# Norms and transposes by column halves in a fused two-block transformer kernel

## The chip, the cores and the metric

The kernel runs on one core of one Trainium2 chip. The metric is the time of one execution on the device in microseconds (us), as the median of several runs; lower is better.

## The reference

Two transformer blocks run one after the other on 256 tokens of 1024 channels, in float32. What matters here is that every product over the 1024 channels is preceded by a normalisation of each token over its channels, and by a transposition into feature form.

```python
h = rmsnorm(x, norm_mix_w) * (1.0 + sc1) + sh1      # stage "mix"
x = x + g1 * (concat(hgrn2(h @ w_in), attention, conv) @ w_out)
h = rmsnorm(x, norm_mlp_w) * (1.0 + sc2) + sh2      # stage "mlp"
x = x + g2 * (square(relu(h @ mlp_w1)) @ mlp_w2)
x = rmsnorm(x, final_norm_w)                        # stage "fin"
for i in range(2):                                  # layers 0 and 1
    x = layer_norm(ALPHA * x + mixer_i(x), ln1_g[i], ln1_b[i])          # "ln1_i"
    x = layer_norm(ALPHA * x + swiglu(x, w1, w3, w2), ln2_g[i], ln2_b[i])  # "ln2_i"
    x = x + sigmoid(x @ ple_w_gate[i] + ple_b_gate[i]) * (p[i] @ ple_w_proj[i])
```

## The kernel before

The residual x lies in SBUF as two token halves of 128 partitions with 1024 columns each (`x[:, t, :]`, t = 0 or 1), and its normalised form in `xn` likewise. The weights come as one stream of tiles of 128 x 2048 float32 (1 MB), five slots deep; SyncE issues them in a fixed order, each into the slot that the products have given free. For precision each product is made of three: ScalarE rounds a tile to `w_hi` (line 1122), VectorE subtracts to get `w_lo` (line 1514), the input is split in the same way into `hT_hi` and `hT_lo` (lines 1531, 1532), and TensorE adds up hi x hi, hi x lo and lo x hi (lines 582, 587, 588). The order of each engine's instructions is written out by hand; counting semaphores link the engines, and a list of the uses of the eight PSUM banks sets the order in which they are filled (`psum_full` counts them one by one).

Ahead of eight of the groups of products stands a seam with always the same steps:

- VectorE computes 1 / root of the mean square (`rstd`, with ScalarE's square root between), then normalises the two token halves with one `tensor_scalar` of 1024 columns each: line 1565 for the RMS norm (stages mix, mlp, fin), line 1946 for the layer norm (ln1 and ln2 of both layers). Each adds one to `xn_ready`.
- TensorE (`to_feature_form`, lines 650 to 662) waits for token half t, then transposes its eight blocks of 128 columns into four PSUM banks, two blocks into each. Bank j holds columns 256 j to 256 j + 255 of both token halves, so it is full when the second half has been transposed into it. Line 657 is the transposition.
- ScalarE (`evacuate`) takes the banks in order and copies each with scale and shift into the arena, two instructions of 256 columns (line 1107; line 1105 in stage ple, which has no scale).
- VectorE (`split_transposed`) takes each pair of chunks that ScalarE has made and splits it (lines 1531 and 1532).
- TensorE starts the first product as soon as the first pair is split, and goes by chunks in the first tile, so that it can follow the splits one by one.

In the seam "ple", between layer 0 and layer 1, there is no normalisation: x itself is transposed, after the last addition of line 2114. In the layer-norm seams VectorE has a weight tile (`lo_ahead(tile, 0)`) to split between normalisation and input split, if it has not done so earlier; behind the input split it splits the next weight tile and then scales and shifts x itself (lines 1956 and 1959; 1903 in stage fin). ScalarE rounds weight tiles ahead (`ahead`) at fixed places between its other work; in stage mix two of them come right before the evacuation (line 1199).

Of the kernel before, what the change touches and what calls it, by code (L numbers as in the profile page):

```python
# [24 lines left out]
ALU = mybir.AluOpType  # L25
# [3 lines left out]
P = 128  # L29
T = 256  # L30
TT = T // P
# [283 lines left out]
def build(nc, x_in, wstream, pcol_in, prow_in, const_in, p_in, out):  # L315
    ctx = ExitStack()
    with ctx:
# [22 lines left out]
        x = sb("x_res", [P, TT, D])  # L340
        xn = sb("xn", [P, TT, D])
# [26 lines left out]
        ident = const[:, CONST["ident"]:CONST["ident"] + P]  # L368
# [91 lines left out]
        stat = tiny[:, 80:96]  # L460
# [8 lines left out]
        mv = tiny[:, 164:172]  # L469
# [17 lines left out]
        psum_full = sem("psum_full")  # L487
# [9 lines left out]
        xn_ready, fin_scaled = sem("xn_ready"), sem("fin_scaled")  # L497
# [56 lines left out]
        def _(pe):  # L554
# [95 lines left out]
            def to_feature_form(stage, n):  # L650

                banks = [begin("tr", stage, j) for j in range(4)]
                for t in range(TT):
                    pe.wait_ge(xn_ready, TT * (n - 1) + t + 1)
                    for j in range(4):
                        for c in range(2):
                            last = nc.tensor.transpose(  # L657
                                banks[j][:, c * T + t * P:c * T + (t + 1) * P],
                                (x if stage == "ple" else xn)[:, t, (2 * j + c) * P:(2 * j + c + 1) * P], ident)
                        if t == TT - 1:  # L660
                            last.then_inc(psum_full, 1)
                chunks(DC)

            def modulation(u):
# [157 lines left out]
            for t in range(TT):  # L822
                K = (t + 1) * P
                for j in range(4):
                    b = begin("sc", t, j)
                    r = 32 * j
                    for hh in range(2):
                        last = mm(b[:, hh * K:(hh + 1) * K],
                                  iqT[r:r + 32, hh * T + t * P:hh * T + (t + 1) * P],
                                  ikT[r:r + 32, 0:K], start=True, stop=True)  # L830
# [6 lines left out]
            for h in range(4):  # L837
                last = mm(b[:, h * P:(h + 1) * P], A_hg[:, h * T:h * T + P], v_hg[:, h * P:(h + 1) * P],
                          start=True, stop=True)
            last.then_inc(psum_full, 1)  # L840
            b = begin("hgo", 1)
            for h in range(4):
                mm(b[:, h * P:(h + 1) * P], A1_hg[:, h * P:(h + 1) * P], v_hg[:, h * P:(h + 1) * P],
                   start=True, stop=False)
                last = mm(b[:, h * P:(h + 1) * P], A_hg[:, h * T + P:(h + 1) * T],
                          v_hg[:, 512 + h * P:512 + (h + 1) * P], start=False, stop=True)
# [3 lines left out]
            for c in range(2):  # L850
# [5 lines left out]
                for j in range(31):  # L856
                    last = mm(b[:, 0:T], tap_matrix(c, j), hpad[:, c * 286 + j:c * 286 + j + T],
                              start=j == 0, stop=j == 30)
# [5 lines left out]
            for c in range(2):  # L864
                last = mm(b[:, 0:T], avg[:, :], conv[:, c * T:(c + 1) * T], start=c == 0, stop=c == 1)
            last.then_inc(psum_full, 1)
            for t in range(TT):
                pe.wait_ge(o_normed, t + 1)
                b = begin("hgt", t)
                for h in range(4):  # L870
                    last = nc.tensor.transpose(b[:, h * P:(h + 1) * P],
                                               q_hg[:, t * 512 + h * P:t * 512 + (h + 1) * P], ident)
# [3 lines left out]
            for c in range(2):  # L876
                last = mm(b[:, 0:T], avg[:, :], conv[:, c * T:(c + 1) * T], start=c == 0, stop=c == 1)
# [41 lines left out]
            for layer in range(2):  # L919
                if layer == 0:  # L920
# [6 lines left out]
                    for j in range(2):  # L927
# [3 lines left out]
                        for c in range(2):  # L931
                            for t in range(TT):
                                last = nc.tensor.transpose(
                                    b[:, c * T + t * P:c * T + (t + 1) * P],
                                    xn[:, t, (2 * j + c) * P:(2 * j + c + 1) * P], ident)
# [15 lines left out]
                    for t in range(TT):  # L951
                        for n in range(2):
                            b = begin("uq", t, n)
                            m = 512 if n == 0 else 256
                            for k in range(2):
                                x_ready(k, 4)
                                last = product3(b[:, 0:m], x_part(k, t * P, (t + 1) * P),
                                                (vh[:, k, n * 512:n * 512 + m], vl[:, k, n * 512:n * 512 + m]),
                                                k == 0, k == 1, first)
# [4 lines left out]
                    for j in range(4):  # L964
                        b = begin("uk", j)
                        for o in range(2):
                            for k in range(2):
                                x_ready(2 + k, 4)
                                c = (2 * j + o) * 64
                                last = product3(b[0:64, o * T:(o + 1) * T], (vh[:, k, c:c + 64], vl[:, k, c:c + 64]),  # L970
                                                x_part(2 + k), k == 0, k == 1, first)
                        last.then_inc(psum_full, 1)
                    for n in range(2):
                        b = begin("uv", n)
                        for t in range(TT):
                            for k in range(2):
                                c = 512 + n * T
                                last = product3(b[:, t * T:(t + 1) * T], x_part(2 + k, t * P, (t + 1) * P),
                                                (vh[:, k, c:c + T], vl[:, k, c:c + T]), k == 0, k == 1, first)
# [3 lines left out]
                    for t in range(TT):  # L983
                        last = nc.tensor.transpose(b[0:96, t * P:(t + 1) * P], krtok[:, t * 96:(t + 1) * 96], ident)
# [502 lines left out]
        def _(dve):  # L1487
            step = [0]
            V = nc.vector
# [30 lines left out]
            def own(s, n=1):  # L1520

                made[s.name] = made.get(s.name, 0) + n
                dve.wait_ge(s, made[s.name])
# [32 lines left out]
            def rms_norm(n, pieces=1):  # L1556
                dve.wait_ge(squares_summed, n)
                squares = ssum[:, 0:TT]
                if pieces > 1:
                    squares = stat[:, 4:4 + TT]  # L1560
                    link(V.tensor_reduce(squares, ssum[:, 0:TT * pieces].rearrange("p (t n) -> p t n", t=TT), AX.X,
                                         ALU.add))
                rstd(TT, 1.0 / D, EPS, squares)
                for t in range(TT):
                    V.tensor_scalar(xn[:, t, :], x[:, t, :], stat[:, 8 + t:9 + t], None, ALU.mult)\
                        .then_inc(xn_ready, 1)
                own(xn_ready, TT)

            def softmax(name, heads, base, bias, scale, c0, beside, tiles):
                us = units(heads)  # L1570
# [367 lines left out]
            def layer_norm(g_row, b_row, stage, layer, tile, pieces):  # L1938

                for t in range(TT):  # L1940
                    last = V.bn_aggr(mv[:, 2 * t:2 * t + 2],
                                     bn[:, 24 * t:24 * t + 6 * pieces].rearrange("p (a b) -> p a b", a=pieces))
                link(last)
                rstd(TT, 1.0, EPS_LN, mv[:, 0:4].rearrange("p (t e) -> p t e", e=2)[:, :, 1])
                for t in range(TT):
                    V.tensor_scalar(xn[:, t, :], x[:, t, :], mv[:, 2 * t:2 * t + 1], stat[:, 8 + t:9 + t],
                                    ALU.subtract, ALU.mult).then_inc(xn_ready, 1)
                own(xn_ready, TT)

                lo_ahead(tile, 0)  # L1950
                split_transposed(stage)
                lo_ahead(tile, 1)
                if g_row == 0:
                    dve.wait_ge(lay_loaded, 16 * (layer + 1))
                for t in range(TT):
                    last = V.tensor_tensor(x[:, t, :], xn[:, t, :], lay_row(g_row), ALU.mult)
                link(last)
                for t in range(TT):
                    last = V.tensor_tensor(x[:, t, :], x[:, t, :], lay_row(b_row), ALU.add)
                link(last)  # L1960

            for layer in range(2):
# [164 lines left out]
                            last.then_inc(x_done, 1)  # L2127
                last = gated(3)
                if layer == 0:
                    last.then_inc(xn_ready, TT)  # L2130
                    own(xn_ready, TT)
                    lo_ahead("ff")
                    split_transposed("ple")
                else:
                    last.then_inc(x_done, 1)
                    own(x_done, 4)
# [134 lines left out]
```

## Time and profile before

| | |
|---|---|
| median of 3 runs | 1299.59 us (1299.54 to 1299.69) |
| profiled execution | 1301.13 us |
| its span, from first to last instruction | 1299.3 us |
| TensorE busy (matmuls) | 1163.6 us, 90% of the span |
| VectorE busy | 754.8 us, 58% |
| ScalarE busy | 546.4 us, 42% |
| granted TensorE clock, mean | 0.934 of full |

The span is what the trace shows of the profiled execution; 1.8 us of its time lie around it. In the rows below PE is TensorE, PEld its weight loads, DVE VectorE, ACT ScalarE; bank, arena, xn and so on are the program's own names of buffers. A granted clock of 1.00 is 2.4 GHz, of 0.50 is 1.2 GHz. What a row calls idle is the time the engine had nothing to run, with the instruction whose end released it.

### The profile page before, as it was taken

The page shows a single profiled execution, that of the slowest core. Times are in us where ns is not written, and L with a number is a line of the kernel's source. Part 1 is how long each engine was busy: PE and PEld are TensorE (multiplying, and loading weights), DVE is VectorE, ACT ScalarE, POOL GpSimd, SP SyncE. Part 2 cuts the span into 40 slices and gives each one's busy share as a digit, 9 for nine tenths or more (in the row PEclk, how much of TensorE's full clock was granted, in tenths as well). Part 3 has the DMA queues.
Part 4 walks back from the last instruction along what each step waited for, and adds up shares of the span by engine and source line. Part 5 has one row for each costly group of instructions (what it writes and reads, how often), then busy time and mean ns, then how long its engine had stood idle before and what let it go on. Part 6 is the DMA issues. An engine that isn't in the chain of part 4 may idle for free.

```text
span 1299.3 us, 18592 instructions
## 1 busy us (share of the span) xinstructions
PE 1163.6 (90%) x7908; PEld 1045.8 (80%) x7908; DVE 754.8 (58%) x932; ACT 546.4 (42%) x755; POOL 0.2 (0%) x4
## 2 busy tenths in 40 slices
PE   4879989779999989947879999987999979999997
PEld 2879778559998879946679998886987659999887
DVE  2565556756775455366575665486344457566557
ACT  4562227244443334384543333344444444333333
POOL 0000000000000000000000000000000000000000
PEclk7788999888999998978999999998998979999999
DMA  9522764123555535410235555535431115455551
GB/s 387 229 83 98 287 229 177 61 90 132 193 180 185 193 128 215 150 66 33 98 118 176 194 176 184 193 130 211 147 114 68 63 67 183 175 193 177 192 182 34
DMA packets 33698, 200.95 MB, mean 155 GB/s; under 512 B 3152, under 2 KB 4688, under 8 KB 11984
## 3 DMA queue, kind: packets, MB, share of 16 engines
q1 hardware_dynamic: 32048, 190.30, 40.3%
q10 hardware_dynamic: 1568, 9.46, 1.9%
q8 instruction: 63, 1.03, 0.3%
q14 instruction: 19, 0.16, 0.0%
HBM read 198.70 MB, written 1.05 MB: 154 GB/s over the span
## 4 chain that ended last, share of the span: by engine, by line
PE 71%; DVE 16%; ACT 6%; DMA 4%; issue 2%; ACTq 0%; SPq 0%; DVEq 0%
PE bank L582 21%; PE bank L587 20%; PE bank L588 20%; DMA raw<-wstream 4%; DVE w_lo L1514 4%; PE bank L771 2%; DVE hT_lo L1532 2%; ACT w_hi L1122 1%; PE bank L1030 1%; DVE hT_hi L1531 1%; PE bank L764 1%; PE bank L1029 1%; PE bank L657 1%; PE bank L706 1%; PE bank L674 1%
## 5 line engine op out<-in xcount | busy, mean ns | idle before, releaser
L1514 DVE TENSOR_TENSOR w_lo<-raw,w_hi 128x2048 fp32r<-128x2048 f32 (+1 forms) x159 | 358.2, 2257 | 191.6 <-ACT w_hi L1122 184.5
L1122 ACT ACTIVATE w_hi<-raw 128x2048 fp32r<-128x2048 f32 (+1 forms) x159 | 299.4, 1885 | 280.0 <-PE bank L582 237.7
L582 PE MATMUL bank<-hT_hi,w_hi 128*128 128x256 f32 (+1 forms) x1360 | 392.5, 289 | 20.0 <-DVE w_lo L1514 11.0
L587 PE MATMUL bank<-hT_lo,w_hi 128*128 128x256 f32 (+1 forms) x1360 | 390.0, 287 | 0.0
L588 PE MATMUL bank<-hT_hi,w_lo 128*128 128x256 f32 (+1 forms) x1360 | 389.5, 286 | 0.0
L582 PEld LDWEIGHTS bank<-hT_hi,w_hi 128*128 128x128 f32 (+1 forms) x1360 | 264.9, 195 | 24.5 <-DVE w_lo L1514 12.5
L587 PEld LDWEIGHTS bank<-hT_lo,w_hi 128*128 128x128 f32 (+1 forms) x1360 | 265.1, 195 | 0.1
L588 PEld LDWEIGHTS bank<-hT_hi,w_lo 128*128 128x128 f32 (+1 forms) x1360 | 264.8, 195 | 0.2
L582 PE MATMUL bank<-w_hi,hT_hi 128*128 128x256 f32 (+3 forms) x448 | 148.3, 331 | 32.0 <-DVE w_lo L1514 12.1
L587 PE MATMUL bank<-w_lo,hT_hi 128*128 128x256 f32 (+3 forms) x448 | 144.3, 322 | 0.0
L588 PE MATMUL bank<-w_hi,hT_lo 128*128 128x256 f32 (+3 forms) x448 | 143.7, 321 | 0.0
L582 PEld LDWEIGHTS bank<-w_hi,hT_hi 128*128 128x128 f32 x448 | 92.6, 207 | 42.7 <-issue 18.6
L582 PE MATMUL bank<-w_hi,hid_hi 128*128 128x512 f32 x304 | 118.3, 389 | 0.0
L587 PE MATMUL bank<-w_lo,hid_hi 128*128 128x512 f32 x304 | 118.3, 389 | 0.0
L588 PE MATMUL bank<-w_hi,hid_lo 128*128 128x512 f32 x304 | 118.3, 389 | 0.0
L588 PEld LDWEIGHTS bank<-w_hi,hT_lo 128*128 128x128 f32 x448 | 92.2, 206 | 5.0
L587 PEld LDWEIGHTS bank<-w_lo,hT_hi 128*128 128x128 f32 x448 | 92.7, 207 | 4.2
L587 PEld LDWEIGHTS bank<-w_lo,hid_hi 128*128 128x128 f32 x304 | 57.1, 188 | 11.8
L582 PEld LDWEIGHTS bank<-w_hi,hid_hi 128*128 128x128 f32 x304 | 57.1, 188 | 11.8
L588 PEld LDWEIGHTS bank<-w_hi,hid_lo 128*128 128x128 f32 x304 | 57.1, 188 | 11.8
L1147 ACT ACTIVATE arena<-arena,tiny 128x128 f32<-128x128 f32 (+1 forms) x56 | 25.0, 447 | 72.0 <-DVE tiny L1592 71.9
L1465 ACT ACTIVATE arena<-bank 128x512 f32<-128x512 f32 x22 | 13.1, 597 | 78.0 <-PE bank L588 78.0
(264 smaller groups left out, 1099.4 us busy)
## 6 DMA issues: line engine op xcount, KB each, us to landing
raw<-wstream SPq DMA_DIRECT2D x179, 1024.0 KB, 4.8
arena<-prow ACTq DMA_DIRECT2D x2, 2560.0 KB, 10.4
x_res<-x ACTq DMA_DIRECT2D x1, 1024.0 KB, 14.5
rows<-prow ACTq DMA_DIRECT2D x2, 512.0 KB, 24.0
out<-x_res SPq DMA_DIRECT2D x4, 256.0 KB, 2.1
const_sb<-const ACTq DMA_DIRECT2D x1, 872.0 KB, 18.6
raw<-wstream SPq DMA_DIRECT2D x1, 768.0 KB, 4.1
raw<-wstream SPq DMA_DIRECT2D x1, 544.0 KB, 3.8
```

Source lines behind the costliest of these rows:

```text
L582: ins = mm(o, a[0], b[0], start=start, stop=False)
L587: mm(o, a[0], b[1], start=False, stop=False)
L588: return mm(o, a[1], b[0], start=False, stop=stop)
L657: last = nc.tensor.transpose(banks[j][:, c * T + t * P:c * T + (t + 1) * P], (x if stage == "ple" else xn)[:, t, (2 * j + c) * P:(2 * j + ...
L674: last = mm(b[32 * g:32 * g + 32, j * T:(j + 1) * T], csil[:, k:k + 1].to_broadcast([P, 32]), w[:, k, :], start=half == 0, stop=half == 1)
L706: last = mm(b[:, i * P:(i + 1) * P], lhsT, rhs, start=True, stop=True)
L771: last = mm(b[par * 64:par * 64 + 64, hh * P:(hh + 1) * P], values(4 * g + par + 2 * hh, m), pT_[:, (hh * nb + m) * P:(hh * nb + m + 1) * ...
L1122: A(w_hi[n % HI][:, 0:m], raw[:, slot % RAW, 0:m], ACT.Copy).then_inc(weights_rounded, 1)
L1147: last = A(L, L, ACT.Exp, bias=negmax[:, m + hh:m + hh + 1], accum_out=rowsum[:, m + hh:m + hh + 1])
L1465: A(act_out[i % 2], b[:, :], ACT.Sigmoid).then_inc(silu_sig_done, 1)
L1514: V.tensor_tensor(w_lo[slot][:, 0:m], raw[:, slot, 0:m], w_hi[n % HI][:, 0:m].bitcast(F32), ALU.subtract).then_inc(weights_split, 1)
L1532: V.tensor_tensor(hT_lo[:, s], src, hT_hi[:, s].bitcast(F32), ALU.subtract).then_inc(input_split, 1)
```

## The change

VectorE normalises columns 0 to 511 of both token halves, then columns 512 to 1023 of both: four instructions of 512 columns in place of two of 1024. Each adds one to `xn_ready`, which so counts four for a seam. TensorE transposes in the same order: blocks for banks 0 and 1 from token half 0, the same from half 1, then those for banks 2 and 3. The number of transposes (16) and their destinations are the same. In the seam ple the order of the transposes changes as well, and the one instruction that releases them adds four.

```diff
@@ to_feature_form
-                for t in range(TT):
-                    pe.wait_ge(xn_ready, TT * (n - 1) + t + 1)
-                    for j in range(4):
-                        for c in range(2):
-                            last = nc.tensor.transpose(
-                                banks[j][:, c * T + t * P:c * T + (t + 1) * P],
-                                (x if stage == "ple" else xn)[:, t, (2 * j + c) * P:(2 * j + c + 1) * P], ident)
-                        if t == TT - 1:
-                            last.then_inc(psum_full, 1)
+                for half in range(2):
+                    for t in range(TT):
+                        pe.wait_ge(xn_ready, 2 * TT * (n - 1) + TT * half + t + 1)
+                        for j in (2 * half, 2 * half + 1):
+                            for c in range(2):
+                                last = nc.tensor.transpose(
+                                    banks[j][:, c * T + t * P:c * T + (t + 1) * P],
+                                    (x if stage == "ple" else xn)[:, t, (2 * j + c) * P:(2 * j + c + 1) * P], ident)
+                            if t == TT - 1:
+                                last.then_inc(psum_full, 1)
@@ rms_norm
-                for t in range(TT):
-                    V.tensor_scalar(xn[:, t, :], x[:, t, :], stat[:, 8 + t:9 + t], None, ALU.mult)\
-                        .then_inc(xn_ready, 1)
-                own(xn_ready, TT)
+                for half in range(2):
+                    for t in range(TT):
+                        s = slice(half * 512, (half + 1) * 512)
+                        V.tensor_scalar(xn[:, t, s], x[:, t, s], stat[:, 8 + t:9 + t], None, ALU.mult)\
+                            .then_inc(xn_ready, 1)
+                own(xn_ready, 2 * TT)
@@ layer_norm
-                for t in range(TT):
-                    V.tensor_scalar(xn[:, t, :], x[:, t, :], mv[:, 2 * t:2 * t + 1], stat[:, 8 + t:9 + t],
-                                    ALU.subtract, ALU.mult).then_inc(xn_ready, 1)
-                own(xn_ready, TT)
+                for half in range(2):
+                    for t in range(TT):
+                        s = slice(half * 512, (half + 1) * 512)
+                        V.tensor_scalar(xn[:, t, s], x[:, t, s], mv[:, 2 * t:2 * t + 1], stat[:, 8 + t:9 + t],
+                                        ALU.subtract, ALU.mult).then_inc(xn_ready, 1)
+                own(xn_ready, 2 * TT)
@@ seam ple
-                    last.then_inc(xn_ready, TT)
-                    own(xn_ready, TT)
+                    last.then_inc(xn_ready, 2 * TT)
+                    own(xn_ready, 2 * TT)
```

## Rows read from the trace of the kernel before

**Rows 1.** The page: span, and TensorE's busy time (share of the span).
```profile
span 1299.3 us, 18592 instructions
PE 1163.6 (90%) x7908; PEld 1045.8 (80%) x7908; DVE 754.8 (58%) x932; ACT 546.4 (42%) x755; POOL 0.2 (0%) x4
```

**Rows 2.** The page: shares of the chain that ended last.
```profile
PE 71%; DVE 16%; ACT 6%; DMA 4%; issue 2%; ACTq 0%; SPq 0%; DVEq 0%
```

**Rows 3.** TensorE's waits, whole span: total us, times, longest us.
```profile
PE bank L657 <- DVE xn L1565: 9.8, 2, 5.1
...
PE bank L657 <- DVE xn L1946: 7.3, 2, 3.9
...
PE bank L657 <- DVE x_res L2114: 3.7, 1, 3.7
```

**Rows 4.** Timeline, seam mlp: start us, length us, engine, line, [idle before <-releaser].
```profile
292.78 1.42 DVE L1565 TENSOR_SCALAR xn<-x_res,tiny 128x1024 f32<-128x1024 f32 x2
...
293.68 3.64 PE L657 MATMUL bank<-const_sb,xn 128*128 128x128 f32 x16 [5.14 <-DVE xn L1565]
296.08 3.76 ACT L1107 ACTIVATE arena<-bank,tiny 128x256 f32<-128x256 f32 x8 [3.60 <-PE bank L657]
297.20 0.43 DVE L1531 CAST hT_hi<-arena 128x512 fp32r<-128x512 f32 x1 [3.01 <-ACT arena L1107]
...
298.50 0.55 PE L582 MATMUL bank<-hT_hi,w_hi 128*128 128x256 f32 x1 [1.18 <-DVE hT_lo L1532]
```

**Rows 5.** The chain in order of time, seams mlp and ln1 of layer 1.
```profile
293.68 2.38 PE bank L657 x10
...
1064.97 0.82 DVE xn L1946
...
1065.93 1.51 PE bank L657 x10
```

**Rows 6.** VectorE's groups by form: busy us, mean ns of one, idle before.
```profile
L1946 DVE TENSOR_SCALAR xn<-x_res,tiny 128x1024 f32<-128x1024 f32 x8 | 6.1, 810 | 0.1
...
L1565 DVE TENSOR_SCALAR xn<-x_res,tiny 128x1024 f32<-128x1024 f32 x6 | 4.2, 750 | 0.1
...
L1973 DVE TENSOR_SCALAR xn<-xn,tiny 128x256 f32<-128x256 f32 x4 | 1.1, 349 | 0.0
```

**Rows 7.** Timeline, seam mix.
```profile
39.07 3.65 PE L657 MATMUL bank<-const_sb,xn 128*128 128x128 f32 x16
...
39.80 3.71 ACT L1122 ACTIVATE w_hi<-raw 128x2048 fp32r<-128x2048 f32 x2 [12.81 <-DVE tiny L1663]
```

**Rows 8.** Timeline, seam ln2 of layer 0.
```profile
853.80 1.91 PE L657 MATMUL bank<-const_sb,xn 128*128 128x128 f32 x16
855.10 3.76 ACT L1107 ACTIVATE arena<-bank,pcol_sb 128x256 f32<-128x256 f32 x8 [4.67 <-PE bank L657]
856.15 0.43 DVE L1531 CAST hT_hi<-arena 128x512 fp32r<-128x512 f32 x1 [1.55 <-ACT arena L1107]
```

**Rows 9.** Timeline, TensorE, second product tile behind fin.
```profile
497.31 0.38 PE L582 MATMUL bank<-w_hi,hT_hi 128*128 128x256 f32 x1 [0.32 <-DVE w_lo L1514]
```

**Rows 10.** TensorE's waits from 660 to 850 us.
```profile
PE bank L582 <- DVE w_lo L1514: 1.7, 1, 1.7
```

**Rows 11.** Timeline, seam ple, VectorE.
```profile
886.35 2.29 DVE L1514 TENSOR_TENSOR w_lo<-raw,w_hi 128x2048 fp32r<-128x2048 f32 x1
...
889.56 0.43 DVE L1531 CAST hT_hi<-arena 128x512 fp32r<-128x512 f32 x1 [0.91 <-ACT arena L1105]
```

**Rows 12.** Windows: us, PE, PEld, DVE, ACT, POOL busy (x), clock, DMA share, GB/s.
```profile
298.50:302.20 3.70, 3.69 (x17) 3.70 (x18) 3.50 (x7) 3.14 (x4) 0.00 (x0) 0.50 0.56 179
302.30:478.00 175.70, 175.70 (x1130) 160.98 (x1130) 104.10 (x84) 67.91 (x49) 0.00 (x0) 1.00 0.51 181
654.00:657.20 3.20, 2.64 (x13) 2.67 (x14) 1.13 (x2) 0.24 (x1) 0.00 (x0) 0.50 0.00 0
886.00:889.30 3.30, 2.83 (x14) 2.86 (x15) 2.61 (x2) 0.43 (x2) 0.00 (x0) 0.50 0.00 0
```

## The prediction

> **What bounds the kernel now.** I read the page first. The span is 1299.3 us and TensorE is busy in 90% of it [rows 1]; of the chain that ended last it has 71%, VectorE 16%, ScalarE 6% [rows 2]. So the kernel is a row of TensorE-bound products, and what can be won is the seams between them. The waits of TensorE say which seams: the transposes of line 657 waited 9.8 us in two places for the RMS normalisation (line 1565), 7.3 us in two for the layer normalisation (line 1946), 3.7 us once for line 2114 [rows 3]. The change does not touch what comes ahead of the normalisation, so most of these waits stay; the question is how long it takes from the first normalisation to the first product behind it.
>
> The timeline of one such seam (stage mlp) shows that [rows 4]. VectorE normalises both token halves from 292.78 on (1.42 us for two instructions), TensorE transposes from 293.68 (16 in 3.64 us), ScalarE starts to evacuate at 296.08, VectorE to split at 297.20, and the first product starts at 298.50. VectorE waited 3.01 us for ScalarE and ScalarE for TensorE: each hand-over is late by the one before it. The chain says what exactly ScalarE waited for: ten transposes, 2.38 us [rows 5]. Bank 0 needs all eight of token half 0 and then two of half 1, as the loop goes over four banks for each token half.
>
> **What the change makes of it.** Bank 0 is full after four transposes of half 0 and two of half 1: six in place of ten. And the first normalisation has 512 columns in place of 1024, so the transposes start earlier. The rest of the chain (two evacuations, cast, subtraction, product) is the same, and each bank's evacuation and split lasts longer than two transposes, so later banks do not become the gate: at mlp bank 2 would be full after fourteen transposes, as now, about 0.3 us before ScalarE comes to it.
>
> Durations. A transpose at the low clock adds (3.64 - 2.38)/6 = 0.21 us [rows 4, 5]; at the high clock 16 last 1.91 us and ScalarE starts 1.30 us after the first [rows 8], so one adds about 0.11. A normalisation of 512 columns is in no row: 256 take 0.349 and 1024 take 0.750 us [rows 6], which by a straight line is 0.48; for the layer normalisation (0.810) I take 0.54, the same 0.27 less. A second one right behind adds 0.08 less (1.42 - 0.75 = 0.67 [rows 4, 6]), so 0.40 and about 0.47. Bounds: not under 0.35 (the row of 256), not over 0.75 (the 1024 one); I take the line because both its ends are operations of this kind. From the end of a normalisation to TensorE's start it takes 0.15 us (293.68 - 292.78 - 0.75). Four then end some 0.4 us later than two. That is hidden: VectorE sits idle about 3 us before its first split [rows 4]. The four waits on the semaphore in place of two come while TensorE has transposes to do, and the pieces of half 1 are ready (0.48 + 0.40 + 0.15 us after the start) before four cold transposes are over (0.63 + 0.85).
>
> Place by place:
> - mix, at 39 us: nothing. The sixteen transposes run 39.07 to 42.72, but ScalarE rounds two weight tiles from 39.80 to 43.51 and evacuates behind them [rows 7]. Its normalisations lie far ahead, under the modulation.
> - mlp: 0.27 + 4 x 0.21 = 1.12 us.
> - fin: the same form and the same low clock, 1.12. Behind it the second product tile waits for VectorE (0.32 us for w_lo) [rows 9], and VectorE's order of work starts from the first split, so it moves by these 1.12 us and takes TensorE with it.
> - ln1 of layer 0: 1.12, by the same rows; a later wait of 1.7 us for w_lo [rows 10] is on VectorE's order and moves too.
> - ln2 of both layers: TensorE is still at the embedding product when the normalisations end, so only the order counts, 4 x 0.11 = 0.44 each, 0.88. Here VectorE does a w_lo tile between normalisations and split; with 0.4 us more before it, it still ends before the arena is evacuated (now VectorE waits 1.55 us for that [rows 8]).
> - ple: no normalisation, only the order: 4 x 0.21 = 0.84. VectorE's w_lo started at 886.35 and takes 2.29, so until 888.65; the split started at 889.56 [rows 11] and can move 0.9. It just fits.
> - ln1 of layer 1: the high clock held for the first transposes, ten lasted 1.51 us and the normalisation began at 1064.97, the tenth ended at 1067.44 [rows 5]. New: second normalisation ready at 1064.97 + 0.54 + 0.47 + 0.15 = 1066.13, two transposes 0.39 (0.11 and the length of a last one, about 0.28), full at 1066.52: 0.92.
>
> Sum: 3 x 1.12 + 0.88 + 0.84 + 0.92 = 6.0 us.
>
> **The clock.** At mlp TensorE runs at the low level, 1.2 GHz (granted 0.50), from before the transposes until 302.2: 17 products in 3.7 us, where the high level (1.00) then holds to 478 with TensorE busy 175.70 of 175.70 us [rows 12]. No wait lies in that stretch, so whatever the clock gives back at mlp reaches the end. Between last transpose and first product TensorE now pauses 1.18 us [rows 4]. New, the transposes end at 293.41 + 3.64 = 297.05 and the product starts at 298.50 - 1.12 = 297.38: a pause of 0.33. At ln1 of layer 0 and at ple the clock rose at 657.2 and 889.3, within 3 us of the first transpose and during unbroken transposes, before any pause [rows 12]; at mlp it took 8.6 us, through a pause. So I expect the shorter pause to let it rise about 3.4 us sooner, as much as the whole low stretch at ple or ln1 (3.2 and 3.3 us of it are in the rows): 3.4 us at half rate is 1.7 us. Bounds: nothing, to 3.7/2 = 1.85 if all products run fast. I take 1.7, nearer the upper one, as the pause nearly vanishes. At fin and the two ln1 seams I take 0 for the clock: there VectorE's w_lo chain sets the third tile, which a faster TensorE would only wait for.
>
> The Trainium skill says otherwise ("TensorE: Matmul & The Clock Gate", Part 4: PE-mode transpose): transposes do not count as activity for the clock. By that rule an unbroken train of them would not raise the clock; here the granted clock rose at 657.2 and at 889.3 with only transposes running, so the trace disagrees. Were it right all the same, the 1.7 us would be missing: rival 1.
>
> **The sum.** 6.0 + 1.7 = 7.7 us. The profiled execution took 1301.13 us with a span of 1299.3; the span would become 1291.6, the execution 1293.4. The median of the runs shown is 1299.59, 1.54 below the profiled one, and the same 7.7 off it gives **1291.9**.
>
> **Rivals.**
> 1. The clock does not rise sooner at mlp (transposes count little, or the pause was not what kept it low). For: at mlp, transposes ran 3.6 us without a rise. Against: ln1 and ple. 1299.6 - 6.0 = 1293.6. Chance 0.17.
> 2. The clock gives back more: from mlp on, all work lies 3 to 7 us earlier against whatever moves the clock, and other low stretches with TensorE busy end one step (1.7 us) sooner. One or two: 1290.2 to 1288.5. Chance 0.13.
> 3. The order helps less than counted, a new gate standing at half the way (VectorE's four normalisations longer than the line says, so that they, and w_lo behind them, hold the split; or ScalarE late with bank 0 for its square-root and weight work). With 512 columns at 0.75 us each the 0.27 is lost and the second piece comes at 1.65 us, which alone takes over 0.5 us a place. Some 3 us left: 1296.6. Chance 0.09.
> 4. The seams are hidden: a shift at one is swallowed by a wait for another cause behind it (a weight transfer, a softmax). Against: no DMA wait appears among TensorE's at these places. 1299 to 1300. Chance 0.07.
> 5. Slower: the clock. New phases put more busy stretches at 1.2 GHz; each step of 3.4 us costs 1.7. To be 0.2% slower it takes more than (6.0 + 2.6)/1.7 = 5 extra steps. Six give 1299.6 - 6.0 + 10.2 = 1303.8. Against it: the change makes TensorE's pauses shorter, never longer. Chance 0.04.
>
> My forecast has 0.50. What a measurement of this kernel can tell from no change is about 0.2%, 2.6 us; so faster is 0.50 + 0.17 + 0.13 + 0.09 = 0.89, same 0.07, slower 0.04. The range takes in the forecast, rival 1 and rival 2 but for its far end, and reaches towards rival 3 without holding it: 1289.0 to 1295.8, which leaves out about 0.2.
>
> **What would show it.** In the chain of the new profile, six transposes stand where ten do, some 1.52 us long at the low clock and 0.9 us before ScalarE at the high. From first normalisation to first product, mlp goes from 5.72 us to 4.6; fin and ln1 likewise; ple's from line 2114 to the first product by 0.8. The 512-column normalisation shows near 0.48 and 0.54. The granted clock at mlp reaches 1.00 near 299. I am wrong if ScalarE at mlp still starts over 3 us after the first normalisation, if the first split waits for VectorE's own work, or if clock stretches elsewhere move by more than the seams do.

## The result and the profile after

The changed kernel takes 1287.38 us (median of 4 runs, 1283.32 to 1288.04) against 1299.57 (4 runs) of the kernel before: a ratio of 0.9903, 95% interval 0.9883 to 0.9922. In two later sets, on two chips, the ratio came out at 0.9911 (0.9892 to 0.9931) and 0.9916 (0.9902 to 0.9929). The forecast was 1291.9, with a range down to 1289.0: the direction was right, the gain of 12.2 us was 1.6 times the forecast 7.7, and the median lies under the range. (Three executions of this study, with and without edits, took 1350, 1788 and 2555 us and are left out of every figure that follows; the one of 1788 us, with a mean granted clock of 0.585, was the profiled one of the first repeat below, whose profile is therefore not used.)

The page of the changed kernel:

```profile
span 1285.9 us, 18606 instructions
...
PE 1151.8 (90%) x7908; PEld 1035.9 (81%) x7908; DVE 756.5 (59%) x946; ACT 546.5 (43%) x755; POOL 0.2 (0%) x4
...
PE 70%; DVE 17%; ACT 6%; DMA 4%; issue 2%; ACTq 0%; SPq 0%; DVEq 0%
```

Against [rows 1] VectorE has 14 instructions more and 1.7 us more work. TensorE has as many as before, yet 11.8 us less busy time: the same matmuls ran faster. That is the first sign that the seams are only part of the story.

Six of the seven seams behind mix did what was forecast, within 0.16 us; the seventh, ln1 of layer 1, gave less. The timeline of mlp in the changed kernel (start, length, engine, line, [idle before <-releaser]):

```profile
291.65 1.67 DVE L1568 TENSOR_SCALAR xn<-x_res,tiny 128x512 f32<-128x512 f32 x4
...
292.29 3.65 PE L658 MATMUL bank<-const_sb,xn 128*128 128x128 f32 x16 [4.87 <-DVE xn L1568]
293.84 3.75 ACT L1108 ACTIVATE arena<-bank,tiny 128x256 f32<-128x256 f32 x8 [2.49 <-PE bank L658]
294.96 0.43 DVE L1532 CAST hT_hi<-arena 128x512 fp32r<-128x512 f32 x1 [1.63 <-ACT arena L1108]
...
296.26 0.55 PE L582 MATMUL bank<-hT_hi,w_hi 128*128 128x256 f32 x1 [0.32 <-DVE hT_lo L1533]
```

From first normalisation to first product it is 4.61 us (5.72 in [rows 4]); TensorE's pause ahead of the product is 0.32 us, forecast 0.33, before 1.18. The chain in order of time has six transposes where ten stood [rows 5]:

```profile
292.29 1.53 PE bank L658 x6
...
480.76 1.53 PE bank L658 x6
...
649.77 1.52 PE bank L658 x6
...
1052.96 1.52 PE bank L658 x6
```

TensorE still waits 9.3 us (in two places) for the RMS normalisation and 7.2 us (in two) for the layer normalisation, where it waited 9.8 and 7.3 [rows 3]: most of these waits stayed, as forecast.

To see where the rest went I cut both traces at the first normalisation of each seam (at ple: the end of the addition ahead of the transposes). Lengths in us, read from the timelines; "again" are second profiles of the same kernels, from a later set (the repeats below):

| stretch | before | before, again | changed | changed, again | difference | seam alone |
|---|---|---|---|---|---|---|
| start to mlp | 292.8 | 290.0 | 291.6 | 290.6 | none | - |
| mlp to fin | 190.6 | 190.6 | 188.5 | 188.5 | -2.1 | 1.11 |
| fin to ln1, layer 0 | 170.2 | 170.1 | 169.0 | 169.0 | -1.3 | 1.12 |
| ln1 to ln2 | 197.1 | 197.2 | 196.0 | 196.0 | -1.1 | 1.12 |
| ln2 to ple | 35.6 | 35.6 | 35.1 | 35.2 | -0.4 | 0.44 |
| ple to ln1, layer 1 | 178.6 | 178.7 | 172.0 | 172.0 | **-6.6** | 1.00 |
| ln1 to ln2 | 196.3 | 196.3 | 196.0 | 196.0 | -0.3 | 0.26 |
| ln2 to end | 38.1 | 38.1 | 37.6 | 37.7 | -0.5 | 0.44 |

The last column is the time from first normalisation (ple: last addition) to first split, before less after. It sums to 5.5 us. From mlp to the end the changed kernel takes 12.3 us less, so 6.8 us came from elsewhere: 1.0 behind mlp, 5.6 in the attention of layer 1 and 0.1 behind fin. The first stretch holds the seam mix, whose first product came at 45.80 us for 45.75: nothing, as forecast. Behind that it differs from profile to profile (285.3 to 293.0 us over all of this study) by more than the seams save.

What the 6.6 us are, the windows show (TensorE, its loads, VectorE, ScalarE, POOL busy, clock, DMA share, GB/s), first before, then changed:

```profile
886.33:1064.97 178.64, 164.07 (x986) 135.40 (x986) 83.51 (x131) 80.02 (x158) 0.00 (x0) 0.92 0.32 115
```
```profile
880.25:1052.27 172.02, 157.71 (x986) 129.85 (x986) 83.14 (x130) 80.11 (x158) 0.00 (x0) 0.95 0.34 120
```

The same 986 matmuls keep TensorE busy 6.4 us less, at a mean clock of 0.95 in place of 0.92. To four digits the means are 0.9151 and 0.9497: 2 x 0.0849 x 178.6 = 30.3 us at half rate before, 2 x 0.0503 x 172.0 = 17.3 changed. That is 13.0 us fewer, and half of it, 6.5 us, is what TensorE's busy time lost. VectorE and ScalarE are unchanged. In the kernel before, four pieces of this stretch ran at 1.2 GHz with TensorE all but wholly busy:

```profile
937.20:943.90 6.70, 6.70 (x29) 6.25 (x30) 3.51 (x6) 4.07 (x11) 0.00 (x0) 0.50 0.45 157
998.60:1005.40 6.80, 6.80 (x25) 4.91 (x24) 3.95 (x8) 3.31 (x11) 0.00 (x0) 0.50 0.01 2
903.10:906.40 3.30, 3.15 (x14) 3.15 (x15) 2.83 (x3) 1.91 (x1) 0.00 (x0) 0.50 0.42 137
1056.70:1060.00 3.30, 3.30 (x10) 2.52 (x9) 2.67 (x4) 2.38 (x3) 0.00 (x0) 0.50 0.76 303
```

In the changed kernel the first of them lasts half as long, and the second has gone; products run at the high level all through where it was:

```profile
929.20:932.50 3.30, 3.30 (x15) 3.08 (x15) 3.02 (x5) 1.01 (x5) 0.00 (x0) 0.50 0.36 89
988.00:1001.00 13.00, 13.00 (x68) 9.31 (x67) 6.98 (x14) 5.75 (x21) 0.00 (x0) 1.00 0.23 82
```

The third and the fourth have gone too, and a new piece of some 3.4 us has come at 1007.7. Behind mlp the products ran low for 1.3 us in place of 3.7 [rows 12]:

```profile
296.30:297.60 1.30, 1.30 (x6) 1.30 (x7) 1.23 (x3) 1.30 (x4) 0.00 (x0) 0.50 0.06 13
297.80:478.00 180.20, 178.56 (x1147) 163.22 (x1145) 109.22 (x91) 70.92 (x54) 0.00 (x0) 1.00 0.50 182
```

So three questions went to the chip: which half of the edit makes the 5.5 us; whether the shorter pause is what raised the clock at mlp; and whether the 5.6 us in layer 1 belong to the seams or to where the work lies against the clock's rises and falls.

### The profile page after: what moved, and what is told of

It reads as the page before. It is cut to its first block, busy times and chain, and to the rows that moved or that the text cites. A ratio compares the mean times of both kernels' runs of the same rounds, so it can differ in the third digit from the quotient of the medians.

```text
span 1285.9 us, 18606 instructions
## 1 busy us (share of the span) xinstructions
PE 1151.8 (90%) x7908; PEld 1035.9 (81%) x7908; DVE 756.5 (59%) x946; ACT 546.5 (43%) x755; POOL 0.2 (0%) x4
## 4 chain that ended last, share of the span: by engine, by line
PE 70%; DVE 17%; ACT 6%; DMA 4%; issue 2%; ACTq 0%; SPq 0%; DVEq 0%
PE bank L582 21%; PE bank L587 20%; PE bank L588 20%; DVE w_lo L1515 5%; DMA raw<-wstream 4%; PE bank L772 2%; DVE hT_lo L1533 2%; ACT w_hi L1123 1%; PE bank L1031 1%; DVE hT_hi L1532 1%; PE bank L765 1%; PE bank L1030 1%; PE bank L675 1%; PE bank L707 1%; DVE x_res L1961 1%
## 5 line engine op out<-in xcount | busy, mean ns | idle before, releaser
L1515 DVE TENSOR_TENSOR w_lo<-raw,w_hi 128x2048 fp32r<-128x2048 f32 (+1 forms) x159 | 358.1, 2257 | 188.6 <-ACT w_hi L1123 181.4
L587 PEld LDWEIGHTS bank<-w_lo,hid_hi 128*128 128x128 f32 x304 | 57.1, 188 | 11.8
```

The costliest lines, as they stand in the source:

```text
L587: mm(o, a[0], b[1], start=False, stop=False)
L1515: V.tensor_tensor(w_lo[slot][:, 0:m], raw[:, slot, 0:m], w_hi[n % HI][:, 0:m].bitcast(F32), ALU.subtract).then_inc(weights_split, 1)
```

## The experiments

Times are medians, and means where runs spread; "ratio" is against the kernel before on the same chip. The kernel before was run 67 times beside the edited ones over the four later sets (mean 1297.9 us, from 1291.7 to 1302.9).

**The same two kernels again.** No edit.

> The changed kernel once more, to see how it spreads. Theory A (the seams save some 5.5 us by themselves and the rest, some 7 us, is the granted clock, whose rises and falls happen to lie differently against the work from run to run): the runs spread over several us, from 1283 to 1290, and in the profile the low stretches lie at other places than in the first profile. Theory B (the clock's share is caused by the new seams alone and is the same each time): all runs within 0.5 us of 1287.5, low stretches at the same places.

1285.2 us, five runs from 1285.1 to 1288.8. The kernel before, 17 runs, 1292.2 to 1301.0. Both spread by several us, the kernel before more than the four runs at 1299.5 had let me think; theory B's 0.5 us is out. Where the low stretches lie needs two more profiles:

> The kernel before, profiled once more. Theory A (layer 1's attention, between the seams ple and ln1, meets the clock's steps where they happen to lie): from ple's first transpose to the first normalisation of ln1 not 178.6 us as in the first profile but elsewhere between 172 and 180. Theory E (the new seams shorten that stage in every run, for a reason other than the position of the steps): 178 us again, and the changed kernel's again 172 to 173.

> The changed kernel, profiled once more. Theory A: from ple's first transpose to ln1's first normalisation anywhere from 171 to 178 us. Theory E: 172 to 173 us. Both: mlp to fin 188.5, fin to ln1 169.0, ln1 to ln2 196.0.

1297.89 us (10 runs) and 1286.97 (4 runs). Layer 1's stretch, first before, then changed:

```profile
883.40:1062.10 178.70, 164.08 (x986) 135.32 (x986) 83.54 (x132) 79.98 (x158) 0.00 (x0) 0.92 0.32 115
```
```profile
879.20:1051.20 172.00, 157.69 (x986) 129.84 (x986) 83.14 (x130) 80.10 (x158) 0.00 (x0) 0.95 0.33 120
```

Within 0.1 us of the first profiles, though the seams came 1 to 3 us earlier after the start. Theory A, as I had put it (anywhere between 172 and 180), is wrong: from mlp on each kernel repeated its own course, and its two profiles differ in the stretch ahead of mlp. Theory E's numbers held. But that it is reproducible does not say that the seams cause it.

**Only the order of the transposes.** Against the changed kernel; the layer norm is edited like the RMS norm.

```diff
-pe.wait_ge(xn_ready, 2 * TT * (n - 1) + TT * half + t + 1)
+pe.wait_ge(xn_ready, 2 * TT * (n - 1) + 2 * (t + 1))
...
+for t in range(TT):
+    V.tensor_scalar(xn[:, t, :], x[:, t, :], stat[:, 8 + t:9 + t], None, ALU.mult).then_inc(xn_ready, 2)
```

> The transposes in the new order, the normalisations in two instructions of 1024 columns as before. Both theories: each seam saves four transposes' time (0.85 us at the low clock, 0.44 at the high one) but not the 0.27 us of the earlier start: from the first normalisation to the first split at mlp, fin and ln1 of layer 0 3.6 us (before 4.4, changed kernel 3.3). Sum of the seams 4.2 us. Theory A: the time lies 4 to 12 us under the kernel before, somewhere from 1287 to 1296. Theory B: close to the changed kernel, 1288 to 1290.

1289.55 us, ratio 0.9939 (0.9920 to 0.9958). First normalisation to first split at mlp, from its timeline:

```profile
289.24 1.42 DVE L1566 TENSOR_SCALAR xn<-x_res,tiny 128x1024 f32<-128x1024 f32 x2
...
292.81 0.43 DVE L1532 CAST hT_hi<-arena 128x512 fp32r<-128x512 f32 x1 [2.16 <-ACT arena L1108]
```

3.57 us, as expected (3.6): 0.85 of the 1.11 are the order. Mlp to fin took 188.6 us, fin to ln1 171.4 (before 190.6 and 170.2): beside the seams, the clock gave 1.1 us at mlp and took 2.1 behind fin. Layer 1's stretch took 172.4.

**Only the pieces, in the old order.** Each pair of banks waits for its piece of token half t; half 0 is normalised wholly before half 1. Against the kernel before; the layer norm likewise.

```diff
+for t in range(TT):
+    for half in range(2):
+        s = slice(half * 512, (half + 1) * 512)
+        V.tensor_scalar(xn[:, t, s], ...).then_inc(xn_ready, 1)
...
+    for j in range(4):
+        pe.wait_ge(xn_ready, 2 * TT * (n - 1) + 2 * t + j // 2 + 1)
```

> The normalisations in pieces of 512 columns, token half 0 wholly before token half 1, and the transposes in the order of before, each pair of banks waiting for its piece. Both theories: only the earlier start is won, 0.27 us in each of the seams mlp, fin and ln1 of layer 0 and layer 1, nothing in ln2 and ple; first normalisation to first split at mlp 4.15 us (before 4.42, changed 3.31). In all 1.1 us, under what the spread of the clock lets a few runs tell.

1293.66 us, ratio 0.9968 (0.9957 to 0.9978), some 4.2 us less than its chip's kernel before by the ratio, four times the 1.1 us. The seam is as expected:

```profile
290.09 1.67 DVE L1567 TENSOR_SCALAR xn<-x_res,tiny 128x512 f32<-128x512 f32 x4
...
294.25 0.43 DVE L1531 CAST hT_hi<-arena 128x512 fp32r<-128x512 f32 x1 [2.48 <-ACT arena L1107]
```

4.16 us (expected 4.15, before 4.42). At ln1 of layer 1, where the clock was now low during the transposes, first normalisation to first split took 4.15 us for 3.62 and not 0.27 less. Mlp to fin is 190.4, with the clock low there as long as before. But layer 1's stretch, whose seam ple is here the one of before, has shrunk:

```profile
883.10:1056.40 173.30, 158.77 (x986) 131.27 (x986) 83.52 (x132) 80.03 (x158) 0.00 (x0) 0.95 0.33 119
```

5.4 us less for an edit that changes no instruction in it: the work merely comes to it 0.5 us sooner after mlp (593.0 us for 593.5). The granted clock runs the same course at first and then stays low for 3.4 us at 934.3, where it stayed low for 6.8 at 937.1 before.

**TensorE's pause filled, nothing else.**

```diff
 b = begin(*key)
+if by_chunk:
+    for _ in range(5):
+        nc.tensor.transpose(b[:, 0:P], xn[:, 0, 0:P], ident)
```

> The kernel before, but in the seams mix, mlp, fin, ln1 and ln2 TensorE does five more transposes into the bank of the first product (overwritten by it) while it waits for the first split, so its pause of 1.2 us between transposes and first product is filled at the low clock. Nothing waits for them. Theory C (the pause keeps the clock low at a seam; the changed kernel gains 1.0 us at mlp because its pause is shorter): from mlp's first normalisation to fin's 189.5 us or less (before 190.5, changed 188.5), fin to ln1 unchanged at 170.0, as VectorE's order sets it. Low stretch at mlp 6.8 us in place of 10.2. Theory D (only the new seams' own shift counts): 190.5 and a low stretch of 10.2 us.

1295.72 us, ratio 0.9977 (0.9963 to 0.9991). The added transposes end as the first split does; the first product starts at 294.55, and from 294.8 on the products run at the high level:

```profile
289.82 3.65 PE L663 MATMUL bank<-const_sb,xn 128*128 128x128 f32 x16 [5.14 <-DVE xn L1571]
...
293.26 1.27 PE L622 MATMUL bank<-const_sb,xn 128*128 128x128 f32 x5
```
```profile
294.90:470.00 175.10, 175.10 (x1135) 160.81 (x1135) 105.25 (x86) 69.13 (x51) 0.00 (x0) 1.00 0.51 182
```

Mlp to fin takes 189.0 us in place of 190.6, with the time to the first split as before (4.43 us): the pause had kept the clock low, and 1.6 us is what that cost (theory C). Behind fin, 1.4 us of it were lost again (171.6 us for 170.2): a low stretch of 3.4 us came at 492.8 that the kernel before doesn't have. I had not expected that. And layer 1's stretch, which holds none of the added transposes:

```profile
882.20:1055.70 173.50, 158.47 (x986) 131.03 (x986) 83.30 (x132) 80.05 (x158) 0.00 (x0) 0.95 0.33 119
```

5.2 us less than before. Together with the run above this is the answer on layer 1: some 5 us can come without the change's seams. It isn't the place of the clock's fall against the start of layer 1 that decides, though: here the clock fell at 881.9, 0.3 us ahead of the end of ple's last addition, and in the kernel before at 885.9, 0.4 us ahead of it, so the two stretches begin alike and part only 54 us later.

**Layer 1 later, by work that does nothing.** VectorE adds constants into a free buffer ahead of the last gated sum. I reckoned 0.45 us for each addition; the traces show 0.33 to 0.36, so the expected 0.9, 1.8 and 2.3 us of delay were 0.7, 1.3 and 1.8 (length of ln2 to ple, against the same kernel without). Two of them in the kernel before and in the changed one, then four in the changed, five in the one before.

```diff
+if layer == 0:
+    for i in range(2):
+        V.tensor_tensor(xn[:, i % 2, 0:T], ones[:, 0:T], ones[:, 0:T], ALU.add)
 last = gated(3)
```

> The kernel before with two idle VectorE additions (0.9 us in all) ahead of the last gated sum at the seam ple, so that all of layer 1 comes 0.9 us later. Theory A: layer 1 meets the clock's steps elsewhere, as it did in the changed kernel; the low stretches of layer 1 with TensorE busy shrink, and the time is LESS than before in spite of the added work, by up to 5 us (1295 to 1300), or at least not 0.9 us more. Theory B: 1300.5, 0.9 us more than before.

> The changed kernel with the same 0.9 us ahead of layer 1. Theory A: part of the clock's gain in layer 1 is lost or won, the time differs from the changed kernel's by anything from -3 to +6 us, and not by 0.9. Theory B: the changed kernel plus 0.9 us, 1288.3.

> The changed kernel with four idle VectorE additions (1.8 us in all) ahead of layer 1. Theory F (the stretch from ple to ln1 depends on where the clock's last fall lies against ple's first transpose: it takes 178 us where the fall comes 0.4 to 1.1 us ahead of the transpose, as in the kernel before, and 172 to 174 elsewhere): the delay moves the changed kernel into that place (0.7 us), so ple to ln1 takes 177 us and the time is about 1293.5, 7 us more than the changed kernel for 1.8 us of work. Theory E (the shorter seams themselves shorten that stretch): 172 us, and 1288.3.

> The kernel before with five idle VectorE additions (2.3 us) ahead of layer 1. Theory F: the fall lies outside the bad place, ple to ln1 takes 173 to 174 us in place of 178.6, and the time is 1295 to 1296, some 2.5 us LESS than the kernel before for 2.3 us more work. Theory E: 178.6 us, and 1300.3.

```profile
885.14 1.88 DVE L2130 TENSOR_TENSOR xn<-ones 128x256 f32<-128x256 f32 x5
```

| kernel | measured delay | runs | mean | kernel before, its chip, mean | ple to ln1 in the profile | of it at the low clock |
|---|---|---|---|---|---|---|
| before + 0.9 us | 0.7 | 12 | 1297.0 | 1297.7 | 177.9 | 33.0 |
| before + 2.3 us | 1.8 | 12 | 1296.4 | 1297.7 | 175.1 | 25.1 |
| changed + 0.9 us | 0.7 | 6 | 1288.3 | 1297.7 | 173.8 | 20.5 |
| changed + 1.8 us | 1.3 | 7 | 1288.2 | 1297.7 | 169.4 | 9.9 |

With two additions the kernel before is as fast as without (ratio 0.9998, 0.9984 to 1.0011), which a plain cost of 0.7 us would fit as well. With five it is too (0.9990, 0.9974 to 1.0006), and there 1.8 us at face value would be 1.0014, outside that interval: layer 1's stretch is 3.5 us shorter where it begins 1.8 us later. The changed kernel's means of 1288.3 and 1288.2 are what theories B and E had put down (1288.3 both times). They lie about 2 us above its means without (1286.5, 1286.2 and 1286.9 in its three sets), which six or seven runs don't set apart from a plain cost. What the profiles show is that the length of this stretch, with the same 986 matmuls, goes with its time at the low clock: from 169.4 us with 9.9 low to 178.6 with 30.3. My rule for it (theory F) is refuted. It put the changed kernel with 1.8 us at 177 us and 1293.5. The clock did fall where the rule wanted it, at 874.6, 0.4 us ahead of the end of ple's last addition at 875.0, just as in the kernel before, but the profile has 169.4, the shortest of all without warming,

```profile
875.00:1044.40 169.40, 155.67 (x986) 128.85 (x986) 83.40 (x130) 79.86 (x158) 0.00 (x0) 0.97 0.34 122
```

in an execution of 1279.7 us, while the six others took 1287.7 to 1290.6. Of the 9.2 us that part it from the profiled execution with two additions, 5.2 lie ahead of mlp (285.3 us for 290.5), so it is an unusual execution from its first stretch on. What makes the clock's course a good or a bad one I can't say from these runs.

**The clock held high through the seams (below called warming).** Both kernels, with transposes of the identity while TensorE waits for the normalisation (at ple: for the last addition); bank 0 is overwritten afterwards.

```diff
-banks = [begin("tr", stage, j) for j in range(4)]
+banks = [begin("tr", stage, 0)]
+for _ in range({"mlp": 32, "fin": 32, "ln1_0": 24, "ln1_1": 24, "ple": 24}.get(stage, 0)):
+    nc.tensor.transpose(banks[0][:, 0:P], ident, ident)
+banks += [begin("tr", stage, j) for j in range(1, 4)]
```

> The changed kernel, with TensorE transposing the identity into bank 0 (overwritten after) while it waits for the first normalisation: 32 times at mlp and fin, 24 at ln1 and ple. If that holds the clock high over these four kinds of seam, the transposes and the first products run at 2.4 GHz: from mlp to fin 187 us in place of 188.5, fin to ln1 168.5 for 169.0, ln1 to ln2 195.5 for 196.0. In all 2 to 4 us under the changed kernel, 1283. If the clock falls all the same, the added transposes take 6.8 us at the low level at mlp and delay the seam by up to 2 us each: 1290.

> The kernel before with the same added transposes of the identity while TensorE waits (32 at mlp and fin, 24 at ln1 and ple), the order and the normalisations as before. If they hold the clock high, the seams themselves shorten: first normalisation to first split at mlp 3.4 us (before 4.42, with both edits 2.64), as ten transposes then take 1.3 us; mlp to fin 188.0 us in place of 190.6. The new order is then worth less: 0.7 us a seam in place of 1.1. Theory A' (layer 1's stretch goes by the position of the clock's steps, not by the order of the transposes): ple to ln1 is not 178.6 us but 170 to 175, and the time is 1284 to 1290, at least as good as the changed kernel though the change is not in it. Theory E: ple to ln1 178 us less what the seam saves, and 1293.

The changed kernel with it takes 1280.91 us (6 runs, 1279.6 to 1289.1), ratio 0.9877 (0.9853 to 0.9902): faster than the kernel before, and by some 0.3% than the changed one (0.9903 to 0.9916), whose intervals it still overlaps. Its timeline at mlp:

```profile
285.25 3.65 PE L654 MATMUL bank<-const_sb 128*128 128x128 f32 x32
...
289.63 1.67 DVE L1571 TENSOR_SCALAR xn<-x_res,tiny 128x512 f32<-128x512 f32 x4
...
290.26 1.94 PE L661 MATMUL bank<-const_sb,xn 128*128 128x128 f32 x16 [1.35 <-DVE xn L1571]
291.14 3.76 ACT L1111 ACTIVATE arena<-bank,tiny 128x256 f32<-128x256 f32 x8 [1.82 <-PE bank L661]
292.27 0.43 DVE L1535 CAST hT_hi<-arena 128x512 fp32r<-128x512 f32 x1 [0.96 <-ACT arena L1111]
```

The sixteen transposes take 1.94 us in place of 3.65, the seam up to the split 2.64 in place of 3.31, and mlp to fin 187.2 us (188.5). Ln1 to ln2 took 195.4 us as expected, but fin to ln1 170.0, where I had expected 168.5 and the changed kernel takes 169.0. From mlp to the end it is 990.0 us against 994.3. The kernel before with it takes 1289.7 us (five runs), ratio 0.9933 (0.9918 to 0.9948), with 170.7 us for layer 1's stretch, 1.0 of the saving being its shorter seam ple; that is in the range of theory A', though it isn't as fast as the changed kernel (1285.2 to 1287.4). First normalisation to first split at mlp was 3.34 us (expected 3.4). Mlp to fin took 189.4 us, not the 188.0 I expected: the clock still fell, later, over the first products,

```profile
296.90:300.20 3.30, 3.30 (x17) 3.30 (x16) 3.16 (x5) 1.78 (x1) 0.00 (x0) 0.50 0.86 318
```

here with the old order's long pause (1.80 us at the high level), while the changed kernel with warming has no low stretch there:

```profile
289.63:476.90 187.27, 184.96 (x1200) 169.48 (x1200) 114.46 (x104) 75.97 (x66) 0.00 (x0) 1.00 0.48 175
```

By the two ratios the change is still worth 0.56%, some 7 us (about 3.5 to 11 by their intervals), on top of the warming, and from mlp to the end the profiles say 7.0 too (997.0 and 990.0). The seams alone give 3.7 of that (0.70 us at mlp, fin and both ln1, 0.43 at ln2, nothing at ple); the rest is the clock again.

## Why the prediction was right and wrong

- **Bound and chain.** Right: all five waits of the transposes stayed, and the seams shrank by the hand-over to ScalarE, ten transposes becoming six. The runs with the order alone and the pieces alone confirm the two halves of the sum, 0.85 and 0.26 us at mlp (expected 0.85 and 0.27).
- **The sum of the seams.** Forecast 6.0, measured 5.5. The straight line for 512 columns was good: 0.480 and 0.543 us as the medians (forecast 0.48 and 0.54). mlp, fin and ln1 of layer 0 1.11 to 1.12 (1.12); ln2 0.44 (0.44); ple 1.00 (0.84), as the first transposes met the high clock and the split went straight behind w_lo, the limit I had put at 0.9. There the sign "the first split waits for VectorE's own work" came true, at no loss against the forecast. ln1 of layer 1 was the term mis-sized, 0.26 for 0.92: the first transposes had run at the high level before, and I had kept that for the new ones; they ran low (six in 1.52 us), since the clock now fell 0.2 us ahead of the normalisation. Rival 3's "over 0.5 us a place" was also reckoned wrong where the clock is low: with 0.75 us for a first piece, four transposes would end at 0.75 + 0.15 + 0.85 = 1.75 us, behind the second piece at 1.65, so 0.27 a place was at stake. The pieces took 0.48 us, so it never arose.
- **The cover.** Right: VectorE's four instructions and the additional waits cost nothing, and the gains behind fin and ln1 passed through VectorE's order of work: -1.3 and -1.1 us with seams of 1.12. The clock rose 5.3 us behind fin's first normalisation in place of 10.0 and still gave only 0.1 to 0.2 us there, as forecast: TensorE waited for w_lo instead.
- **The clock at mlp.** The mechanism was right, as the run with the filled pause shows: the pause between transposes and products kept it low. The size was off, 1.0 us for the forecast 1.7, by a slip in the working. The rise did come 3.4 us sooner, 6.0 us behind the first normalisation in place of 9.5. But 1.1 us of that is the seam's own shift, which stood in the 6.0 already: the products at the low level shrink only from 3.8 to 1.4 us, 2.4 us at half rate, 1.2 us. What the Trainium skill states ("TensorE: Matmul & The Clock Gate", Part 4: PE-mode transpose), that transposes don't count as activity for the clock, again disagrees with the traces: with warming, the granted clock of the changed kernel stayed at 1.00 at mlp over 7.8 us in which TensorE ran nothing but transposes and waited between them; without it the clock fell 0.8 us ahead of the normalisation.

```profile
285.70:293.50 7.80, 5.14 (x46) 4.70 (x44) 5.36 (x13) 4.00 (x11) 0.00 (x0) 1.00 0.01 2
```

- **What failed: the clock beyond mlp.** The sum counted it as nothing, and rival 2 (chance 0.13, one or two steps of 1.7 us) as a possibility. It was 13.0 us less at the low level in one stretch, from ple to ln1 of layer 1, nearly four steps net, worth 5.6 us beside the seam; so the sign "clock stretches elsewhere move by more than the seams do" came true. I had seen that all work from mlp on would move by 3 to 7 us against the clock, and gave that no term. The profile of before showed the size of what lay there: four pieces of layer 1, 20 us in all, ran at the low level with TensorE busy, so up to 10 us could be won. It didn't show which way a shift would go: the kernel before with two additions had more of that stretch low (33.0 us for 30.3), with five less (25.1). Why it went down in the changed kernel stays open.
- **The base.** I trusted three runs within 0.15 us of each other. Over 67 later runs the kernel before spreads from 1291.7 to 1302.9. Against their mean of 1297.9 the changed kernel's runs (means 1286.5, 1286.2 and 1286.9 in three sets) gain 11.4. Against the wider base the gain still lies well above the forecast 7.7. The claim that 0.2% can be told from no change was too bold for a few runs.

What stays open: why the change's seams, the pieces alone and the filled pause each took some 5 us off layer 1's stretch. That its length goes with the granted clock is shown, and so is that the seams aren't needed; that the new place of the work against the clock's falls is the cause is only argued. Three kernels came to ple with the clock's fall 0.3 to 0.4 us ahead of the end of the last addition and took 178.6, 173.4 and 169.4 us from there. Open too is what makes the falls keep their place from mlp on in two profiles of a kernel, 1 to 3 us apart at mlp. Only one execution per set is profiled, and of changed + 1.8 us only the one that was unlike the rest.

## What to carry to other kernels

Where one engine's pieces feed a chain of hand-overs, order them so that the first consumer's unit is complete first: six transposes in place of ten, with pieces of half the size, cost nothing and gave 0.3 to 1.1 us at each of seven seams, 5.5 us in all. Reckon a TensorE pause with its aftermath at 1.2 GHz, and look for busy stretches at a granted clock under 1: an edit upstream may free or fill them, and that can be worth more than the edit. When a small edit gains more than its sum, cut both traces at fixed instructions and compare stretch by stretch, and add a delay that does nothing: here 1.8 us of it were free.

## What was not expected of the hardware

- A delay of 1.8 us on the path left the mean of 12 runs where it was (ratio 0.9990, 0.9974 to 1.0006); in the profile the stretch behind it had 25.1 us at the low clock in place of 30.3 and was 3.5 us shorter.
- Five transposes in a 1.2 us pause, whose result is thrown away, let TensorE's clock rise 3.6 us earlier (5.9 us behind the first normalisation, 9.5 before). 32 in a wait of 5 us kept it high through the seam mlp in both kernels, and in the changed one all the way to fin (granted clock 1.00, 0.98 without them); in the kernel before it fell 6 us behind the first normalisation, over products.
- Two profiles of one kernel, taken in different sets, agreed within 0.1 us on each of the seven stretches from mlp to the end, and differed by 1 to 3 us on the first.
